# Two-layer transformer and RWKV kernel on one core: the twelve bias lines as one 96-row product, one write, and four reads in two groups of heads

## What is computed

```
table_a = rel_bias_table[:, :A_HEADS]        # 32 buckets x 8 heads
table_b = rel_bias_table[:, A_HEADS:]        # 32 buckets x 4 heads
h = rms_norm(x, mix_norm_g); proj = h @ w_in
...
logits = q @ k.T * scale + bias_ht[h, rel_bucket(t - s)]   # -1e30 where s > t
p = softmax(logits)
```

## Time and profile before

| | us |
|---|---|
| median of 3 runs (lowest, highest) | 1180.93 (1180.62, 1181.59) |
| span of the profiled execution | 1175.5 |
| PE busy | 1127.3 (96%) |
| DVE busy | 746.6 (64%) |
| ACT busy | 570.9 (49%) |
| POOL busy | 76.0 (6%) |
| bias writes (3 x 768 KB), median to landing | 4.4 |
| bias reads, to landing: 768 KB, 1536 KB | 5.5, 14.1 |

### The profile page before, as it was taken

How to read it: one execution, slowest core, us unless ns; L and a number is a source line. 1 busy time by engine, 2 the same in 40 slices (tenths; PEclk the granted TensorE clock), 3 DMA queues, 4 the chain that set the end, 5 groups by cost and what they waited for, 6 DMA issues and landing times.

```text
span 1175.5 us, 22572 instructions
## 1 busy us (share of the span) xinstructions
PE 1127.3 (96%) x9889; PEld 1071.8 (91%) x9889; DVE 746.6 (64%) x997; ACT 570.9 (49%) x761; POOL 76.0 (6%) x137
## 2 busy tenths in 40 slices
PE   7999999999999999999799999999998989999998
PEld 7787879879999999988688999999986789999998
DVE  4656867357465556767888756555587675665563
ACT  5445556344444434585345544343475554544443
POOL 2221011100000000400000000000020000000000
PEclk9999999999999999999899999999999999999999
DMA  6953354424555555534000555455554215455551
GB/s 253 337 160 108 144 180 180 149 102 173 179 187 180 180 183 193 192 141 144 1 3 3 184 180 188 180 180 184 190 201 143 73 60 188 183 180 180 181 189 61
DMA packets 30238, 185.04 MB, mean 157 GB/s; under 512 B 3579, under 2 KB 6848, under 8 KB 9148
## 3 DMA queue, kind: packets, MB, share of 16 engines
q1 hardware_dynamic: 24464, 174.07, 41.2%
q0 software_dynamic: 2464, 7.11, 2.1%
q10 hardware_dynamic: 3212, 2.42, 0.7%
HBM read 180.18 MB, written 3.41 MB: 156 GB/s over the span
## 4 chain that ended last, share of the span: by engine, by line
PE 75%; DVE 9%; ACT 6%; issue 4%; DMA 3%; POOL 2%; ACTq 0%; SPq 0%; DVEq 0%; POOLq 0%
PE bank L664 74%; ACT w_hi L2184 2%; DVE w_lo L1411 2%; DMA w_raw<-in_weights 2%; ACT exps L2284 1%; DMA bias<-bias_rows 1%; DVE stats L1606 1%; PE bank L843 1%; DVE logits L1598 1%; DVE inverse L2074 0%; PE bank L678 0%; DVE inverse_t L2099 0%; DMA bias_rows<-bias_lines 0%; POOL inverse_rms_diagonals L2672 0%; PE bank L1105 0%
## 5 line engine op out<-in xcount | busy, mean ns | idle before, releaser
L1411 DVE TENSOR_TENSOR w_lo<-w_raw,w_hi 128x2048 fp32r<-128x2048 f32 x160 | 364.8, 2291 | 194.7 <-ACT w_hi L2184 194.5
L2184 ACT ACTIVATE w_hi<-w_raw 128x2048 fp32r<-128x2048 f32 x164 | 312.0, 1913 | 110.7 <-DMA w_raw<-in_weights 105.2
L664 PE MATMUL bank<-x_channels_hi,w_hi 128*128 128x256 f32 x1424 | 231.7, 286 | 9.1 <-ACT w_hi L2184 3.5
L664 PE MATMUL bank<-x_channels_lo,w_hi 128*128 128x256 f32 x1424 | 229.1, 284 | 0.0
L664 PE MATMUL bank<-x_channels_hi,w_lo 128*128 128x256 f32 x1424 | 221.0, 278 | 0.0
L664 PEld LDWEIGHTS bank<-x_channels_hi,w_hi 128*128 128x128 f32 x1424 | 196.8, 192 | 12.5 <-ACT w_hi L2184 3.8
L664 PEld LDWEIGHTS bank<-x_channels_lo,w_hi 128*128 128x128 f32 x1424 | 194.9, 191 | 0.0
L664 PEld LDWEIGHTS bank<-x_channels_hi,w_lo 128*128 128x128 f32 x1424 | 191.5, 189 | 0.0
L664 PE MATMUL bank<-hidden_hi,w_lo 128*128 128x256 f32 x528 | 103.3, 284 | 0.0
L664 PE MATMUL bank<-hidden_hi,w_hi 128*128 128x256 f32 x528 | 102.0, 280 | 0.0
L664 PE MATMUL bank<-hidden_lo,w_hi 128*128 128x256 f32 x528 | 101.7, 279 | 0.0
(11 more groups left out here) (436 smaller groups left out, 1546.8 us busy)
## 6 DMA issues: line engine op xcount, KB each, us to landing
w_raw<-in_weights SPq DMA_DIRECT2D x164, 1024.0 KB, 4.8
bias_rows<-bias_lines POOLq DMA_DIRECT2D x3, 768.0 KB, 4.4
mem_rows<-in_mem POOLq DMA_DIRECT2D x2, 1024.0 KB, 5.2
bias<-bias_rows ACTq DMA_DIRECT2D x1, 1536.0 KB, 14.1
xn<-in_x SPq DMA_DIRECT2D x1, 1024.0 KB, 4.9
out<-xn SPq DMA_DIRECT2D x4, 256.0 KB, 2.5
wide_masks<-in_triangle_masks POOLq DMA_DIRECT2D x1, 832.0 KB, 6.5
bias<-bias_rows ACTq DMA_DIRECT2D x1, 768.0 KB, 5.5
```

The source lines that it names most:

```text
L664: return nc.tensor.matmul(out, lhs, rhs, start=start, stop=stop)
L1411: V.tensor_tensor(k.w_lo[:, s, :], k.w_raw[:, s, :], k.w_hi[:, s, :].bitcast(F32), ALU.subtract).then_inc(k.lo_done, 1)
L2184: A.activation(k.w_hi[:, s, :], k.w_raw[:, s, :], ACT.Copy).then_inc(k.hi_done, 1)
```

## The change

- The split table gets 8 copies of its 12 columns (33 x 96), so that two products give 96 rows: 8 copies of the 12 lines, in one PSUM bank.
- ACT alone copies them out, once (96 x 384), waits for its own copy, and issues one transfer that writes each of the 96 rows 16 times: 128 copies of 12 lines, laid out copy by copy, as many bytes as before. POOL's three transfers and DVE's and ACT's twelve copies are gone.
- ACT then waits for that one transfer, and issues four reads instead of two: both tiles of the "a" heads, then both of the "b" heads, each group with a semaphore of its own. DVE's first addition and POOL's loads wait for group "a" alone.
- DVE's low part of unit 2 no longer stands between its copies.

```diff
@@ tensor_program
-    for h in range(NH):
-        b = bank[2 + h % 6]
...
-        matmul(b[:, 0:RL], k.tab_hi[:, h:h + 1].to_broadcast((NB, P)), k.hot_r[:, :], True, False)
-        matmul(b[:, 0:RL], k.tab_lo[:, h:h + 1].to_broadcast((NB, P)), k.hot_r[:, :], False, True).then_inc(k.bias_made.sem, 1)
-    PE.wait_ge(*k.line_v.at("heads", 3))
-    PE.wait_ge(*k.line_a.at("heads", 3))
+    matmul(bank[2][0:LINE_COPIES * NH, 0:RL], k.tab_hi[:, :, :].rearrange("b c h -> b (c h)"), k.hot_r[:, :], True, False)
+    matmul(bank[2][0:LINE_COPIES * NH, 0:RL], k.tab_lo[:, :, :].rearrange("b c h -> b (c h)"), k.hot_r[:, :], False,
+           True).then_inc(k.bias_made, 1)
+    PE.wait_ge(*k.dve_once.at("mixcols", 0))
+    PE.wait_ge(k.line_kept, 1)
     channel_product("in1", 0, X)
-    PE.wait_ge(*k.line_a.all("heads"))
+    PE.wait_ge(*k.x_gained.all("mix"))
+    PE.wait_ge(*k.x_kept.all("mix"))
@@ vector_program
-                        V.wait_ge(k.io_bias, 32)
+                        V.wait_ge(k.io_bias[tag], 32)
...
-    for h in range(0, NH, 2):
-        V.wait_ge(*k.bias_made.at("heads", h))
-        V.tensor_copy(k.line[:, h, :], bank[2 + h % 6][:, 0:RL]).then_inc(k.line_v.sem, 1)
-        if h == 4:
-            lo(k.of["in1"][0][0] + 1)
+    lo(k.of["in1"][0][0] + 1)
@@ scalar_program
-    for h in range(1, NH, 2):
-        A.wait_ge(*k.bias_made.at("heads", h))
-        A.activation(k.line[:, h, :], bank[2 + h % 6][:, 0:RL], ACT.Copy).then_inc(k.line_a.sem, 1)
+    A.wait_ge(k.bias_made, 1)
+    A.activation(k.line[:, :], bank[2][0:LINE_COPIES * NH, 0:RL], ACT.Copy).then_inc(k.line_kept, 1)
+    A.wait_ge(k.line_kept, 1)
+    nc.scalar.dma_start(k.toep.rearrange("j q r -> q j r"),
+                        k.line[:, :].unsqueeze(1).to_broadcast((LINE_COPIES * NH, P // LINE_COPIES, RL))).then_inc(k.io_lines, 16)
     product("in0", 1)
     product("in1", 0)
-    A.wait_ge(k.io_lines, 16 * NH // 4)
-    for tile, (at, n) in enumerate(((P, P), (0, S))):
-        skew = bass.AP(k.toep.tensor, P - 1 + at, [[RL - 1, P], [P * RL, NH], [1, n]])
-        nc.scalar.dma_start(k.bias[:, :, tile * P:tile * P + n], skew).then_inc(k.io_bias, 16)
+    A.wait_ge(k.io_lines, 16)
+    for tag, h0, h1 in (("a", 0, A_HEADS), ("b", A_HEADS, NH)):
+        for tile, (at, n) in enumerate(((P, P), (0, S))):
+            skew = bass.AP(k.toep.tensor, P - 1 + at + h0 * RL, [[NH * RL - 1, P], [RL, h1 - h0], [1, n]])
+            nc.scalar.dma_start(k.bias[:, h0:h1, tile * P:tile * P + n], skew).then_inc(k.io_bias[tag], 16)
@@ gpsimd_program
-    for h in range(0, NH, 4):
-        G.wait_ge(*k.line_v.at("heads", h // 2 + 1))
-        G.wait_ge(*k.line_a.at("heads", h // 2 + 1))
-        nc.gpsimd.dma_start(k.toep[h:h + 4, :, :].rearrange("h p r -> p h r"), k.line[:, h:h + 4, :]).then_inc(k.io_lines, 16)
-    G.wait_ge(k.io_lines, 16 * NH // 4)
-    G.wait_ge(k.io_bias, 32)
+    G.wait_ge(k.io_bias["a"], 32)
```

More of the change, by code:

```diff
@@ L218, in signals @@
         self.io_lines = nc.alloc_semaphore("bias_lines_written")
-        self.io_bias = nc.alloc_semaphore("bias_loaded")
+        self.io_bias = {tag: nc.alloc_semaphore(f"bias_loaded_{tag}") for tag in ("a", "b")}
         self.io_const = nc.alloc_semaphore("constants_loaded")
@@ L393, in memory @@
         self.tab, self.hot = work("bias_table", 34, [NB, NH]), work("bias_one_hot", 35, [NB, RL])
[L394 removed]
+        self.tab_hi = work("bias_table_hi", 34.125, [NB, LINE_COPIES, NH], F32R)
+        self.tab_lo = work("bias_table_lo", 34.5, [NB, LINE_COPIES, NH], F32R)
         self.hot_r = work("bias_one_hot_r", 37, [NB, RL], F32R)
[L396 to L397 removed]
+        self.toep = nc.dram_tensor("bias_rows", (P // LINE_COPIES, LINE_COPIES * NH, RL), F32, kind="Internal").ap()
+        self.line, self.bias = work("bias_lines", 32, [LINE_COPIES * NH, RL]), work("bias", 64, [P, NH, 384])
         self.proj = work("proj", 40, [P, NT, 2 * 512])
@@ L912, in tensor_program @@
     kept("in1")
-    PE.wait_ge(*k.line_v.all("heads"))
-    PE.wait_ge(*k.line_a.all("heads"))
     def beside_a(i):
@@ L2333, in scalar_program @@
     A.wait_ge(k.io_table, 32)
-    A.activation(k.tab_hi[:, :], k.tab[:, :], ACT.Copy).then_inc(k.act_once.sem, 1)
+    A.activation(k.tab_hi[:, :, :], k.tab[:, :].unsqueeze(1).to_broadcast((NB, LINE_COPIES, NH)), ACT.Copy).then_inc(k.act_once.sem, 1)
     A.activation(k.hot_r[:, :], k.hot[:, :], ACT.Copy).then_inc(k.act_once.sem, 1)
```

19 lines of the change are left out of this document (5 added, 14 removed).

## The result

| | us, median (range) | ratio to the kernel before, 95% interval |
|---|---|---|
| before | 1180.78 (1179.04 to 1181.59) | |
| after | 1191.46 (1191.24 to 1193.10) | 1.0091 [1.0077, 1.0104] |
| forecast | 1182.3 [1178.8 to 1186.0] | |

The changed kernel is 10.7 us slower, 9.2 more than forecast and 5.5 outside the range. Its profiled execution has a span of 1190.3 us. In every run 1.3 to 1.4 us lie outside the span, and not 5.4, as the note under the table of the time before has it: the profiled execution of before (1175.5, so some 1176.8 in all) was simply shorter than any of that kernel's timed runs, of which the lowest is 1178.88. So the two spans differ by 14.8 and the medians by 10.7; the medians decide.

A forecast was written before the change was run, and what follows sets the result against it. Bound by the bias read's chain to `in3`, closely followed by ACT's and DVE's row behind the writes' landing. Span 1175.5 + 1.4 = 1176.9, and 5.4 more for the median: 1182.3 us, range 1178.8 to 1186.0.

The forecast's parts named there:

- PE's part: On PE, 24 bias products become 2 and `in1` is finished at 38.65 instead of 44.27, a gain of 5.6 us.
- The mechanism: PE stands 5 to 7 us ahead of `in2` for qT_a, the clock falls, and the first addition waits for PE.
- The four issues: Issuing four bias reads holds ACT for 2.0 us, 0.7 more than before, within 1.6 to 3.2.
- The write: ACT's single bias write lands at 37.2, near the old 36.95, costing 0.3 us.
- The rival's 39.1: Write lands at 39.1 because unit 6's load is served beside it on all engines; part of a rival with chance 0.23.
- By turns of packets alone: If DMA engines alternate queues packet by packet, unit 6's load takes its turn at once and the write lands at 37.9.
- That reading of the earlier trace: Unit 7's load, issued at 44.47 amid a bias read, came through only when the read was nearly done.
- One clock fall of 1.6 us: PE's 6.0 us stall ahead of `in2` drops its clock once, costing 1.6 us; no second fall at `in3`.
- The sum: Whole kernel: 0.3 (write) + 0.7 (issues) + 1.6 (clock) - 1.2 (slack) = +1.4 us.
- ACT's row gets longer: Late write at 39.1 and issues holding ACT 3.2 us delay unit 5's high part: 1185.4 us, chance 0.23.

## Why the prediction was wrong

- **PE's part**: right. Two products, 0.62 us of waiting, `in1` at full clock, done 13.3 us after the first bias product; the working had 13.1.
- **The mechanism**: right. PE waits ahead of `in2` for qT_a, behind unit 5's high part on ACT, the clock falls there, and the first addition waits for PE and not for the bias.
- **The four issues**: the step that failed. Sized 2.0 us from the 410 and 790 ns of the earlier trace rows, with 3.2 as the end; 6.85 measured, 4.85 too little. The working looked at what an issue costs and at the number of pieces, and named blocking only in its rival, with 3.2 us still as its end. With no load beside them the issues took 3.18.
- **The write**: put at 11.7 us after the first bias product; 14.6 measured, 2.9 too little. The rival's 39.1, 13.6, was nearer. The size of the data phase was taken from the old packets (5.95 us of all engines, where this write's are 6.7 to 7.4), and unit 6's load was held to give way, on the earlier trace rows. By turns of packets alone the working had 37.9, 12.4 us after the first bias product, so that rule alone would not have closed the gap either: 10.55 us of the 13.46 are the write with nothing beside it.
- **That reading of the earlier trace rows**: wrong. The load issued at 44.47 showed 4 packets until 47 because a load takes some 3 us to show any beside a busy queue, and by then the read was nearly done. It didn't give way. The load before it, in the same trace, could have told: issued at 38.34, it moved 46 packets against the read's 47 from 43 to 44 us. The rule of packets in turn, set aside there, holds, and it says the reverse of what was concluded: loads of 8 KB packets push aside reads of 1 KB.
- **One clock fall of 1.6 us**: the fall was 2.1 us (7.71 from `in2`'s start to the logits, 5.65 before), and a second one, 1.56, came in `in3` behind a wait of 2.15. The earlier trace rows had 2.84 us there without a fall, so the length of one wait doesn't tell.
- **The sum**: 2.9 (write) + 4.85 (issues) + 0.45 (first fall) + 1.56 (second) = 9.8 us more than the forecast's +1.4, so +11.2; and PE, behind the second fall, stands 43.9 - 34.3 + 1.6 = 11.2 later. The medians differ by 10.7. That the two agree to 0.5 us is in part luck, since the two profiled executions, counted from the first bias product, differ by 16.3 us in the end.
- **The rivals**: "ACT's row gets longer" was the right one and had 0.23, but at 1185.4. It was priced from rows in which no load was in flight ahead of the reads, though the working itself had found that PE frees unit 2's buffer 6 us sooner. It followed that load to the write and not on to the reads, and unit 7's not at all.

## What to carry to other kernels

An engine that finishes sooner starts its next loads sooner: list every transfer that a freed buffer sets off, and ask what it will meet, down to the last small transfer in the stretch. Don't let an engine that feeds the critical path wait for a transfer and issue the next one; if it must, put the work that others wait for ahead of that wait. And when a removal gains nothing, look for the copy that stands behind the late thing in an in-order row: here 0.9% slower became 0.2 to 0.3% faster by changes of order alone.

## What the runs showed of the hardware

- An issue on ACT's queue is not a fixed cost: 0.37 to 5.34 us for the same kind of read. It was long, 1.8 us and more, for the third of four reads in close order or the second of 1536 pieces wherever a weight load of SP's queue had been issued ahead of the reads or with them: 0.40, 0.60, 5.04 and 0.72 in one row of four.
- Two queues share the engines by packets, not bytes: 103 packets of the load and 99 of the read in 2 us, 0.71 against 0.10 MB.
- A weight load's first packets came about 1 us after its issue into idle engines (issued at 24.17, 20 packets from 25 to 26) and some 3 us after it beside a busy queue (issued at 40.21, none until 43).
- The same 2.36 MB cost the engines 5.95 us in 576 packets from GpSimd's queue and, by an estimate from two stretches, 6.7 to 7.4 us in 1536 packets of 1536 bytes from ACT's.
- During 11 us of transposes the granted clock stayed up (1.00 from 38 to 48 us); 1.84 us of waiting followed, and it still fell once inside `in2` (0.74 over 50 to 54 us).
